# A hybrid pooling and S5 block on one core: x squared before the exponential, a K tile transposed sooner, low weights ahead of low h, and sixteen unread products at the start

## The reference

```python
mod = jax.nn.silu(c) @ w_ada + b_ada
shift, scale, gate = jnp.split(mod, 3, axis=-1)
h = rmsnorm(x, norm_pre) * (1.0 + scale[:, None, :]) + shift[:, None, :]
proj = h @ w_in
u_pool, z_pool, u_ssm, z_ssm, g_pool, g_ssm = jnp.split(proj, list(IN_SPLITS), axis=-1)
y_pool = causal_pool_mixer(u_pool, pool_w, pool_scale) * jax.nn.silu(z_pool)
y_ssm = s5_mixer(u_ssm, a_re, a_im, log_dt, ...) * jax.nn.silu(z_ssm)
merged = (jax.nn.sigmoid(g_pool) * (y_pool @ w_branch_pool)
          + jax.nn.sigmoid(g_ssm) * (y_ssm @ w_branch_ssm))
out = merged @ w_out
return x + gate[:, None, :] * rmsnorm(out, norm_post)
```

## Time and profile before

| | |
|---|---|
| median of three runs | 953.89 us |
| lowest and highest | 953.86, 953.91 us |
| span of the profiled execution, first to last instruction | 951.7 us |
| TensorE busy | 930.3 us, 98% |
| VectorE busy | 640.0 us, 67% |
| ScalarE busy | 347.6 us, 37% |
| GpSimd busy | 45.4 us, 5% |

### The profile page before, as it was taken

One profiled execution on the slowest core, in us unless ns is written; L12 is line 12 of the kernel. 1 busy time (PEld: TensorE's weight loads), 2 busy tenths in 40 slices (PEclk: granted clock), 3 DMA queues, 4 the chain that ended last, 5 costly groups with the idle time before them and its releaser, 6 DMA issues.

```text
span 951.7 us, 11609 instructions
## 1 busy us (share of the span) xinstructions
PE 930.3 (98%) x4408; PEld 781.6 (82%) x4408; DVE 640.0 (67%) x916; ACT 347.6 (37%) x453; POOL 45.4 (5%) x82
## 2 busy tenths in 40 slices
PE   4999999999999999999999999999999999999997
PEld 4888888888888888888888888888888888888885
DVE  5988999877788887437898789665344444455232
ACT  6741353334444444434444436441022221223111
POOL 0019700000000000000000000000000000000000
PEclk9999999999999999999999999999999999999999
DMA  9843355446555444556898582597643268422222
GB/s 352 299 153 125 124 200 166 156 159 195 174 188 202 147 176 152 191 131 183 228 245 224 132 205 88 165 339 262 182 161 107 89 228 202 144 89 89 89 88 89
DMA packets 95719, 164.60 MB, mean 173 GB/s; under 512 B 38576, under 2 KB 55088, under 8 KB 95664
## 3 DMA queue, kind: packets, MB, share of 16 engines
q1 hardware_dynamic: 85872, 159.31, 52.1%
q10 hardware_dynamic: 9792, 4.56, 1.9%
HBM read 116.64 MB, written 47.19 MB: 172 GB/s over the span
## 4 chain that ended last, share of the span: by engine, by line
PE 97%; DVE 1%; ACT 1%; DMA 1%; issue 0%; ACTq 0%; DVEq 0%
PE ps L1948 49%; PE ps L2068 20%; PE ps L2190 9%; PE psb L2068 8%; PE ps L2139 2%; PE psb L2119 2%; PE psb L2128 2%; PE psa L2107 2%; PE psa L2026 1%; PE psa L1948 1%; DMA par_are<-in_a_re 1%; PE psb L2026 0%; PE psb L1976 0%; ACT gt L1028 0%; DVE mod_out L1400 0%
## 5 line engine op out<-in xcount | busy, mean ns | idle before, releaser
L1948 PE MATMUL ps<-bop,w_hi 128*128 128x512 f32 x1120 | 300.6, 390 | 0.9 <-DVE bop L1442 0.9
L1948 PEld LDWEIGHTS ps<-bop,w_hi 128*128 128x128 f32 x1120 | 209.3, 188 | 44.0 <-issue 1.1
L1948 PE MATMUL ps<-bop,w_lo 128*128 128x512 f32 x560 | 172.3, 389 | 0.0
L1948 PEld LDWEIGHTS ps<-bop,w_lo 128*128 128x128 f32 x560 | 105.1, 188 | 21.8
L1396 DVE TENSOR_TENSOR w_lo<-raw,w_hi 128x1024 fp32r<-128x1024 f32 x43 | 53.3, 1239 | 46.9 <-ACT w_hi L1014 46.7
L2068 PE MATMUL ps<-bop,r_hi 128*128 128x512 f32 x272 | 83.7, 389 | 0.0
L1014 ACT ACTIVATE w_hi<-raw 128x1024 fp32r<-128x1024 f32 x43 | 45.3, 1053 | 68.7 <-PE ps L1948 56.3
L2068 PEld LDWEIGHTS ps<-bop,r_hi 128*128 128x128 f32 x272 | 51.1, 188 | 10.6
L2068 PE MATMUL ps<-t_hi,r_hi 128*128 128x512 f32 x140 | 55.1, 393 | 0.0
L2068 PE MATMUL ps<-t_hi,r_lo 128*128 128x512 f32 x140 | 54.5, 390 | 0.0
L2068 PE MATMUL ps<-t_lo,r_hi 128*128 128x512 f32 x140 | 54.5, 389 | 0.0
(11 more groups left out here) (318 smaller groups left out, 1575.4 us busy)
## 6 DMA issues: line engine op xcount, KB each, us to landing
raw<-in_wstream SPq DMA_DIRECT2D x52, 512.0 KB, 5.1
pair_raw<-in_wstream SPq DMA_DIRECT2D x26, 512.0 KB, 4.2
ada<-in_w_ada SPq DMA_DIRECT2D x16, 512.0 KB, 11.2
x_tok<-in_x SPq DMA_DIRECT2D x8, 512.0 KB, 6.8
gs_d<-gt SPq DMA_DIRECT2D x8, 512.0 KB, 5.1
win_d<-win_new SPq DMA_DIRECT2D x8, 512.0 KB, 2.7
wout_d<-wout_new SPq DMA_DIRECT2D x8, 512.0 KB, 3.8
wout<-wout_d SPq DMA_DIRECT2D x8, 512.0 KB, 4.7
```

The costliest lines, as they stand in the source:

```text
L1948: last = mm(ps[slot(u)][:, f * HALF:f * HALF + HALF], a[:, k, :], b(k, f), start=k == order[0] and q == 0, stop=k == order[-1] and q == 2)
```

## The change

`exp` is cut in two: `exp_front`, its first five instructions, and `exp_back`, its last eleven. VectorE squares tile 2 of x first; `exp_front` stands behind it, ahead of the first variance, and `exp_back` behind the square sum of tile 5, ahead of the second. The two angle products move behind the last `split_h`. ScalarE takes `xt_out(2)` ahead of `split_hi(0)`, and `xt_out(3)` ahead of `h_of(0)`. TensorE transposes K tile 5 ahead of `step(0, 0)`; in each `step` the order is now high by high, low weights by high h, high weights by low h, and only the last waits for the low part. Ahead of all, TensorE multiplies two blocks of tile 0 of x sixteen times into `psa`, which nobody reads.

```diff
-        def exp(steps, out_, in_, width):
+        def exp_front(steps, in_, width):
...
             do(stt(r, k, 2.12194440054690583e-4, r, ALU.mult, ALU.add))
+
+        def exp_back(steps, out_, in_, width):
...
         def plain_angles(steps):
 
             do, tt, ts = steps.do, nc.vector.tensor_tensor, nc.vector.tensor_scalar
-            exp(steps, par["dt"], par["ldt"], G)
...
+            xt_out(2)
             split_hi(0)
-            xt_out(2)
+            xt_out(3)
             h_of(0)
             h_high(0)
-            xt_out(3)
             split_hi(1)
...
-            dve.wait_ge(par_in, 16 * 3)
-            plain_angles(steps)
             for half_ in range(2):
...
                     square_sum(t)
+                dve.wait_ge(par_in, 16 * 3)
+                if half_ == 0:
+                    exp_front(steps, par["ldt"], G)
+                else:
+                    exp_back(steps, par["dt"], par["ldt"], G)
...
             split_h(KT - 1)
+            plain_angles(steps)
             reduced_angles(steps)
...
-                pe.wait_ge(h_done, k + 1)
-                last = k_step(u, k, *h)
+                pe.wait_ge(h_hi_done, k + 1)
+                hi, lo = (wx_hi, wx_lo) if n == 2 else (w_hi[n % 2], w_lo[n % 2])
+                h_hi, h_lo = h
+                for q, (a, b) in enumerate(((hi, h_hi), (lo, h_hi), (hi, h_lo))):
+                    if q == 2:
+                        pe.wait_ge(h_done, k + 1)
+                    for f in range(2):
+                        last = mm(ps[slot(u)][:, f * HALF:f * HALF + HALF], a[:, k, :], b(k, f),
+                                  start=k == 0 and q == 0, stop=k == KT - 1 and q == 2)
...
+            pe.wait_ge(tile_in[0], 16)
+            for n in range(16):
+                mm(psa[:, (n % 8) * P:(n % 8) * P + P], x_tok[:, 0, 0:P], x_tok[:, 0, P:2 * P], start=True, stop=True)
...
             transposed(4, range(CH))
+            transposed(5, range(CH))
             step(0, 0)
-            transposed(5, range(CH))
             step(1, 0)
```

More of the change, by code:

```diff
@@ L528, in rounded @@
             steps.do(nc.vector.tensor_scalar(out_, out_, MAGIC, None, ALU.subtract))
-        def exp(steps, out_, in_, width):
+        def exp_front(steps, in_, width):
             do = steps.do
-            tt, stt, ts = nc.vector.tensor_tensor, nc.vector.scalar_tensor_tensor, nc.vector.tensor_scalar
+            stt, ts = nc.vector.scalar_tensor_tensor, nc.vector.tensor_scalar
             k, r, p, q = (wide[z][:, 0:width] for z in ("k", "r", "p", "q"))
@@ L538, in exp @@
             do(stt(r, k, 2.12194440054690583e-4, r, ALU.mult, ALU.add))
+        def exp_back(steps, out_, in_, width):
+            do = steps.do
+            tt, stt, ts = nc.vector.tensor_tensor, nc.vector.scalar_tensor_tensor, nc.vector.tensor_scalar
+            k, r, p = (wide[z][:, 0:width] for z in ("k", "r", "p"))
             c = [1.0, 1 / 2, 1 / 6, 1 / 24, 1 / 120, 1 / 720]
@@ L546, in exp @@
             do(stt(out_, in_, -87.0, p, ALU.is_ge, ALU.mult))
+        def exp(steps, out_, in_, width):
+            exp_front(steps, in_, width)
+            exp_back(steps, out_, in_, width)
         def plain_angles(steps):
             do, tt, ts = steps.do, nc.vector.tensor_tensor, nc.vector.tensor_scalar
-            exp(steps, par["dt"], par["ldt"], G)
             do(tt(wide["ang"][:, 0:G], par["aim"], par["dt"], ALU.mult))
```

## The result

The changed kernel takes **957.36 us** (median of five runs, 956.79 to 958.34 us), the kernel before 953.86 us (953.36 to 953.91 us): a ratio of 1.004, with a 95% interval of 1.0029 to 1.005. It is slower by 3.5 us, where 0.8 us were forecast, and outside the forecast's range.

What follows compares the result with a forecast made beforehand. TensorE, busy 930.3 of 951.7 us, was taken as the bound; 0.63 us (later `step(1, 0)`) plus 0.2 us (GpSimd overlap) made 0.8 us, so span 952.5 us and median 954.7 us, range 953.3 to 956.4 us.

Steps and rivals of the forecast that it cites:

- The first variance: VectorE and ScalarE at the head: first variance at 10.94 us, 1.75 us sooner than 12.69 us.
- the second: Second variance, behind `exp_back` on VectorE: at 17.21 us, 0.49 us later than before, with the chain behind it.
- The 0.6 us of the order: Queues up to `step(1, 0)`: the new order starts it at 29.8 instead of 29.17 us, 0.63 us later.
- (a): Second variance: VectorE is not what it waits for, 16.2 to 16.7 us; 953.5 to 954.1 us, chance 0.13.
- (b): Ahead of `step(1, 0)`: `h_of(1)` comes early enough, 1.8 us gained; 952.1 us or a little below, chance 0.04.
- (d): Transposes: the products do not raise the clock, or end late; 954.7 to 955.2 us, chance 0.07.
- (c): Between the transpose halves: TensorE's clock falls in the pause, K tile 3 1.6 us later; 956.3 us, chance 0.11.
- the sentence on the end of the program: Argument against a clock fall: last product near 945.5 us, clock still 1.00 up to 949.5 us, 4 us of rest.
- the second pause: TensorE ahead of `step(1, 0)`: waits 2.4 us for `h_of(1)`, from 27.4 to 29.8 us.
- The 0.2 us for GpSimd beside VectorE: Half products near 135 us: GpSimd overlaps VectorE's steps 1 us longer; between nothing and 0.5 us, 0.2 taken.
- The wait for the coefficients: ScalarE's wait for the stored coefficients: ends at 125.0 instead of 123.44 us, the angles being 1.6 us late.
- it just fits: Coefficients at 125.0 us come ahead of VectorE's need for the first half weight at 125.7 us.

Runs made afterwards that it cites:

- b1: The kernel before with the sixteen unread products alone ahead of the transposes; 954.22 us against 953.91 us.
- e2: The changed kernel with ten more unread products between the first and second half of the transposes; 955.71 us.
- e5: The changed kernel with both pauses filled: ten unread products between the transpose halves, eight ahead of `step(0, 0)`; 956.28 us.
- e1: The changed kernel without the sixteen unread products; 955.60 us.
- g1: The changed kernel with the whole of exp and the angle products moved into time in which VectorE waits; 954.58 us.
- e3: The changed kernel with K tile 5's transposes behind `step(0, 0)` and `xt_out(3)` behind `h_high(0)` again; 954.20 us.
- e7: The changed kernel with eight unread products ahead of `step(0, 0)`, filling the second pause alone; 955.41 us.
- e4: The changed kernel with ten unread products in the first pause, and K tile 5 and `xt_out(3)` back in their old places; 954.47 us.
- h1: The kernel before with tile 2's square sum first, exp cut in two, and K tile 4 transposed twice, the first time unread; 954.31 us.
- b4: The kernel before with the steps' new order alone, low weights by high h ahead of high weights by low h; 953.80 us.
- b2: The kernel before with tile 2's square sum first, exp cut in two and the angle products behind the last `split_h`; 955.51 us.

## Why the prediction was wrong

**Right, by its own steps.** The first variance was forecast at 10.94 us and came at 11.05 us; the second, which the argument turns on, at 17.21 and 17.20 us. The products cost nothing by themselves (b1), the first half ended at 16.5 us, and the second waited, as said, for its diagonal matrices. Where the clock stayed up, `step(1, 0)` came at 29.92 us (e2) and 29.67 us (e5), and at 29.72 us without the products (e1); the sum had 29.8 us. The 0.6 us of the order are shown by these three (0.5 to 0.75 us). Rivals (a), (b) and (d) did not occur; the products did raise the clock. One slip of the text changes nothing: 9.69 plus 1.06 plus 0.19 us make 10.94, not 10.84 us. The read starts 0.1 us before the square ends, so 10.84 us is what the trace has, and the variance followed 0.1 us behind it.

**Wrong: the weight of rival (c), and its size.** The step that failed is the sentence on the end of the program: TensorE had rested for 4 us there before the clock fell, so the pauses that it forecast, 2.7 and 2.4 us (2.30 and 2.08 us measured), were held to be safe, and (c) was given 0.11. One row of one execution was read as a lag. In the changed kernel the first fall came 2.0 us after the last product, the second when work had been taken up again for 0.7 us, and in g1 the same pause passed without one, as one of 2.30 us did in e3 and one of 2.97 us in b1. The mechanism of (c) was the one that happened, with its own number: K tile 3 was forecast 1.6 us late at 24.1 us, and its copy started at 24.14 us. But (c) charged one fall. The prediction saw the second pause (2.4 us forecast, 2.08 us measured), named it in (c) only as an argument against, and put no price on it; it costs another 1.6 us in the profiled execution, and 1.95 us by e7. 954.7 and two falls give 957.9 us, against 957.36 us measured; on the span the terms are 0.63 + 1.6 + 1.6 = 3.8 us, against 3.85 us measured at the last product. With this price in it, (c) would have stood at 957.9 us, and a range that takes in (c) would have held the result.

**Mis-sized or unseen.** The 0.2 us for GpSimd beside VectorE did not show: the half product came at 138.89 us, 3.94 us later than before, so at most 0.1 us more than TensorE's own delay. The wait for the coefficients was forecast at 125.0 us with TensorE 0.6 us late; the changed kernel never met this case, and e5, which did, waited until 127.25 us because the store took 1.9 us longer. The cover that the text called "it just fits" was gone in e3, e4, e7 and h1 too, at 0.2 to 1.0 us each. What I had not seen at all is that the kernel before sits on this chain already, which b4 shows: it was read as bound by TensorE from 29.17 us on, since no wait was listed there.

The Trainium skill's page TensorE: Matmul & The Clock Gate (What's actually happening) says that activity lifts the throttled state and names idleness as what brings it back. The trace of the changed kernel agrees in kind: 0.50 stands in the clock's column behind both pauses. It can't be read as a fall for every pause, since four others of 2 us and more ahead of 36 us passed without one.

## What to carry to other kernels

Work that wakes TensorE early is worth only what the next pause leaves of it: before starting an engine sooner, look where it will then stand still, and price a fall of the clock for every new pause of about 2 us, not for the likeliest alone; six of ten such pauses saw one here. Steps that move out of an engine's way must land in its idle time; here the exponential moved from time nobody needed to the one place where ScalarE, and behind it all of h, waited for it, and an order that keeps a product in hand for the next wait (K tile 5 ahead of `step(1, 0)`) was worth 3.2 us, the clock's part included. A gain at the head is real only when the next shared chain, here angles, GpSimd, store and ScalarE at 135 us, comes sooner too.

## What the runs showed of the hardware

The clock's falls: each lasted 3.4 us at 1.2 GHz (18.5 to 21.9, 32.2 to 35.5 us, 27.5 to 30.9 us in b2). The profiled executions have ten pauses of TensorE of 2 us and more between its first work and 36 us. Six saw a fall: 2.30 and 2.08 us in the changed kernel, 2.08 us in e1 and in e2, 2.31 us in e7, 2.10 us in b2. Four passed without one, with the records behind them at the high rate: 2.05 us behind the unread products of the changed kernel, 2.08 us in g1, 2.30 us in e3, 2.97 us in b1. So the length of the pause alone does not tell, and what else decides, no run here shows. All pauses of 0.95 to 1.9 us passed. The fall came in the pause (the changed kernel's first and e1, 0.3 and 0.2 us before its end) or 0.3 to 0.8 us after TensorE had gone on (e7, the changed kernel's second, b2), so the row that shows the slow work need not be the one behind the pause.

The clock's column of a page says 1.00 until the first change that the trace holds, also where the records are twice as long (second row against the third).

A store of 2.6 MB landed 8.1 us after its issue in thirteen profiles, and 8.4, 8.7 and 10.0 us after it in the three in which an instruction packet was fetched meanwhile.
